# A two-block transformer on one core: two PSUM banks by turns for one accumulation

## The reference

```python
x = x + gt1 * merge_branches(ya, yb, ga, gb, w_pa, w_pb, w_o)   # m @ w_out: 1024 -> 1024
x = x + gt2 * swiglu(h2, w_gate, w_up, w_down)                  # 2816 -> 1024
...                                                             # the second block:
h = h + mix @ w_out[l]
h = h + (silu(gu[..., :D_FF_2]) * gu[..., D_FF_2:]) @ w_down[l]
```

## Time and profile before

| | |
|---|---|
| median of 3 runs | 3452.6 us (3451.89 to 3452.65) |
| span of the profiled execution | 3452.2 us |
| TensorE busy | 3307.5 us, 96% |
| VectorE busy | 1771.3 us, 51% |
| ScalarE busy | 1203.1 us, 35% |
| GpSimd busy | 445.2 us, 13% |
| read from memory | 285.42 MB, 83 GB/s over the span |

### The profile page before, as it was taken

The page is one execution under the profiler, slowest core; times in us unless marked ns, Lnnn a source line. Parts: engine busy times, 40 slices in busy tenths (PEclk is TensorE's granted clock), DMA queues, the critical chain, the costliest instruction groups (busy, mean ns, idle before and its releaser), DMA issues. The chain is left out here.

```text
span 3452.2 us, 49601 instructions
## 1 busy us (share of the span) xinstructions
PE 3307.5 (96%) x20432; PEld 2652.1 (77%) x20432; DVE 1771.3 (51%) x2736; ACT 1203.1 (35%) x2054; POOL 445.2 (13%) x477
## 2 busy tenths in 40 slices
PE   6999999999999999999999999999999998899998
PEld 4887778788888787776887867667888777578886
DVE  5874657654132456655323357654443385744433
ACT  3214762321131222753223333353332332532322
POOL 0211111000000021114500133120000022200000
PEclk9999999999999999999999999999999999999999
DMA  6420013354122122012222321012223220022232
GB/s 243 147 99 18 2 50 141 129 188 141 62 68 68 55 86 68 2 50 89 97 92 94 102 84 58 26 43 92 96 94 104 98 86 3 31 98 92 96 100 80
DMA packets 78265, 290.66 MB, mean 84 GB/s; under 512 B 8672, under 2 KB 9056, under 8 KB 77280
## 3 DMA queue, kind: packets, MB, share of 16 engines
q1 hardware_dynamic: 78048, 287.55, 24.5%
HBM read 285.42 MB, written 2.10 MB: 83 GB/s over the span
## 5 line engine op out<-in xcount | busy, mean ns | idle before, releaser
L459 DVE TENSOR_TENSOR w_low<-ring,w_high 128x1024 fp32r<-128x1024 f32 x418 | 526.7, 1260 | 1351.8 <-ACT w_high L456 1351.2
L494 PE MATMUL ps<-arena_r,w_high 128*128 128x512 f32 x3568 | 1142.1, 385 | 11.1 <-PEq L1517 9.2
L456 ACT ACTIVATE w_high<-ring 128x1024 fp32r<-128x1024 f32 x418 | 442.9, 1060 | 1517.9 <-PE ps L494 1508.8
L494 PEld LDWEIGHTS ps<-arena_r,w_high 128*128 128x128 f32 x3568 | 646.1, 188 | 163.7 <-issue 16.7
L494 PE MATMUL ps<-low,w_high 128*128 128x512 f32 (+1 forms) x2448 | 764.7, 361 | 0.0
L494 PE MATMUL ps<-high,w_high 128*128 128x512 f32 x2368 | 737.0, 362 | 15.0 <-DVE low L992 7.0
L494 PE MATMUL ps<-high,w_low 128*128 128x512 f32 x2368 | 730.7, 359 | 0.0
L494 PE MATMUL ps<-arena_r,w_low 128*128 128x512 f32 (+1 forms) x1456 | 545.6, 387 | 0.0
L494 PEld LDWEIGHTS ps<-low,w_high 128*128 128x128 f32 x2448 | 411.7, 189 | 74.8 <-issue 1.1
L494 PEld LDWEIGHTS ps<-high,w_high 128*128 128x128 f32 x2368 | 395.2, 188 | 95.8 <-issue 12.0
L494 PEld LDWEIGHTS ps<-high,w_low 128*128 128x128 f32 x2368 | 395.0, 188 | 70.3
(11 more groups left out here) (353 smaller groups left out, 2905.8 us busy)
## 6 DMA issues: line engine op xcount, KB each, us to landing
ring<-in_weights SPq DMA_DIRECT2D x428, 512.0 KB, 3.3
arena<-in_ada_rows SPq DMA_DIRECT2D x80, 512.0 KB, 3.9
arena<-in_ada SPq DMA_DIRECT2D x16, 512.0 KB, 15.5
arena<-in_cond_rows SPq DMA_DIRECT2D x3, 1024.0 KB, 5.8
xL<-in_x SPq DMA_DIRECT2D x1, 2048.0 KB, 10.9
out<-xL SPq DMA_DIRECT2D x4, 512.0 KB, 2.7
low_f<-in_low_rank SPq DMA_DIRECT2D x3, 512.0 KB, 4.2
const<-in_const SPq DMA_DIRECT2D x1, 1104.0 KB, 5.4
```

Of the source, the lines that this page charges most:

```text
L456: act.activation(w_high[:, slot, :], ring[:, place, :], ACT.Copy).then_inc(unit_high.sem, 1)
L459: dve.tensor_tensor(w_low[:, slot, :], ring[:, place, :], w_high[:, slot, :].bitcast(F32), ALU.subtract).then_inc(unit_free.sem, 1)
L494: mm = pe.matmul(bank(4 * (t % 2) + 2 * p + s, width), w, g.split[k][s][x], start=(n == 0 and m == 0), stop=(n == len(part) - 1 and m == 2))
```

## The change

In a `Residual` stage with tokens alone the flag `two_sums` is set. Each tile's products then go by turns into the tile's first bank and the one behind it (0 and 1, or 4 and 5): `turn` counts products times three, the first product in each bank starts an accumulation and the last two end the two. VectorE adds the first bank to the stream as before, waits for that instruction through its chain semaphore, and adds the second bank in the same way. `left_v` is raised by the second.

```diff
                 for m, (w, x) in enumerate(((hi_w, 1), (hi_w, 2), (lo_w, 1))):
+                    if g.two_sums:
+
+                        turn = 3 * n + m
+                        mm = pe.matmul(bank(4 * (t % 2) + 2 * p + turn % 2), w, g.split[k][0][x],
+                                       start=(turn < 2), stop=(turn >= 3 * len(part) - 2))
+                        continue
                     for s, width in g.segs:
...
                     g.made, g.own = made, 0 if made else len(g.split)
+                    g.two_sums = evict.two_sums and len(g.segs) == 1
...
         class Evict:
+            two_sums = False
...
         class Residual(Evict):
+            two_sums = True
...
                     ins = dve.scalar_tensor_tensor(x, bank(4 * (c % 2) + s, w), gate, x, ALU.mult, ALU.add)
+                    if g.two_sums:
+                        chain_v.link(dve, ins)
+                        ins = dve.scalar_tensor_tensor(x, bank(4 * (c % 2) + 1), gate, x, ALU.mult, ALU.add)
                 ins.then_inc(left_v.sem, 1)
```

## The result

The changed kernel takes 3458.8 us (median of 21 runs, 3453.23 to 3463.12) against 3451.75 us (21 runs, 3448.31 to 3456.46): 1.0020 times the time before, 95% interval 1.0014 to 1.0027. That is +7.05 us, at the very edge of what was called no change. The forecast was 3457.0 us and +4.4 us, counted from 3452.6 us, the median of the first three runs.

The account below looks back on a forecast made before the run. TensorE, busy 96% of the span, was taken as the bound; pace 0, inner tiles 0 and stage ends 0.78 + 0.78 + 2.1 + 0.73 = 4.4 us on 3452.6 gave 3457.0 us, range 3442 to 3463.

Parts of the forecast that it names:

- no change: Whole kernel: a difference within about 0.2%, 6.9 us; the forecast of +0.13% fell here, chance 0.67.
- Pace unchanged: TensorE in the six stages: switching banks adds 0 per matmul, tile periods stay 5.60 and 15.40 us.
- Steady alternation saves: Rival, 2160 matmuls: 6 to 7 ns less each, 3443 us (chance 0.12), or all 20 ns, 3414 us (0.03).
- steady alternation costs: Rival, 2160 matmuls: accumulation starts in another bank add up to 2 ns each, 3461.3 us or more; chance 0.16.
- The surplus of the pairs of the earlier trace: Token-and-context matmuls alternating banks: about 13 ns surplus each in place of 20, hinting at a 15 us gain.
- Second evictions of the inner tiles free: Tiles 0 to 6, 42 of 48 added evictions: hidden beside matmuls, cost 0; 30 us if uncovered.
- The six ends: Last tile of each changed stage: second eviction delays what follows, 0.78 + 0.78 + 2.1 + 0.73 = 4.4 us.
- the three straight ends: Second block, TensorE going straight into the next stage: late operands of k = 6 and 7, +0.70 us each.
- the program's end: After the last down projection, final norm and output follow the second eviction in one chain: +0.73 us.
- L1105's wait: TensorE's wait for GpSimd after layer 1's down projection: 2.28 us before, expected to become 3.1 us.
- The clock: Rival: longer TensorE idling after layer 1's down projection brings 1.2 GHz, some 2 us, 3460 us; chance 0.02.
- the likeliest case: Whole kernel: matmul pace unchanged and all stage ends paid, 3457.0 us, by itself 3454.5 to 3459.5; chance 0.59.

Follow-up runs that it names:

- the kernel with the banks alone: Changed kernel with products alternating between two banks but the second bank never added to the stream: 3452.49 us, ratio 1.0000.
- the halves: Kernel before, each six-stage matmul split into two of 256 columns: 3458.29 us in one bank, 3451.37 us by turns, beside 3448.91 us.
- the filler: Changed kernel plus three unread matmuls in TensorE's idle time, two before the final norm, one before layer 1's norm: 3457.47 us, ratio 1.0014.
- the order that removes it: Changed kernel; at four ends VectorE does last-tile evictions and two low operand parts before splitting the next stage's second weight unit: 3453.27 us, ratio 1.0001.

## Why the prediction was right, point by point

*Pace unchanged.* Right, and for the reason given: the switch at a tile's end in the trace before was the experiment in small. Periods to the hundredth, and the kernel with the banks alone at a ratio of 1.0000. "Steady alternation saves" (0.15 together) and "steady alternation costs" (0.16) are both refuted. The surplus of the pairs of the earlier trace rows, the one argument for a gain, was smaller per matmul because their matmuls are shorter, as the halves show, and not because the bank changes. The Trainium skill's N / 2.4 + 2.5 ns ("TensorE: Matmul & The Clock Gate", Back-to-back issue gap), which that section calls the gap of an isolated matmul, gives an estimate of 109.2 ns for 256 columns. The traces have 116.7, with or without a change of bank, so what it leaves out is not the bank.

*Second evictions of the inner tiles free.* Right: no cost for 42 of 48 (ratio 1.0000, 0.9991 to 1.0009).

*The six ends, 4.4 us.* Right as a mechanism, and in size by its readings: 0.79 us at layer 1's norm (first distance with the filler), 0.77 us at its down projection, 0.70 us at each of the three straight ends (0.70 forecast; 0.68 and 0.72 by the table), 0.72 us at the program's end where the clock held. That the stall sits behind VectorE's weight split is shown by the order that removes it. One sign was misread: I expected L1105's wait (now L1111) to grow to 3.1 us. It stayed at 2.26, since the stall before k = 6 and 7, 0.39 us idle and slower restarts, falls into the same stretch and uses it up.

*The clock.* This is the term that was mis-sized. I gave it 0.02 and called it small, by one idle gap of 0.64 us around 1614 that had done no harm. Measured are 0.56 us at layer 1's norm in each of six profiles, in a stretch that begins at that very place, 0.9 to 1.7 us at the end in three of six, and a mean clock lower by 0.0009. At the place that I had named for it, layer 1's down projection, the clock is low before as well (0.90 in the 35 us from 1990 us before, 0.91 after). The page's slices of 86 us, on which I leaned, can't show a stretch of a few us.

*A term that was missing.* The instructions of VectorE in layer 1's norm took 0.2 to 0.5 us longer beside GpSimd, at full clock. The sum had priced this end as a shift of an unchanged chain.

With the chains, 4.4 + 0.56 + about 0.3 + half of 1.6 us are some 6.1 us of the 7.05. The rest was not separated; it is small against the interval of the difference (4.8 to 9.3 us).

*Class and range.* +7.05 us lies just beyond the 6.9 us that I took for the bound of no change; the likeliest case's own range (3454.5 to 3459.5) held the time, but partly by luck. The difference was 2.6 us larger than its sum, and the forecast had started from a median of three runs that was 0.85 us above that of the 21.

## What to carry to other kernels

Before trying to hide a per-instruction surplus, find in the old trace an instance of the one thing the edit changes (here a switch of bank, through two tile lengths and two equations), and what the surplus scales with. Work that is free in the middle of a stage is paid in full in its last tile, where the next stage's operands hang on it; price ends one by one, allow for the clock that a longer idle stretch may cost, and look at what stands ahead of the last eviction in the engine's own order. A time that fits is not yet a cause: cut the stretch in two at the moment when the clock falls, and see how much was lost before it. When an experiment fails, read its trace before dropping the theory: it may have moved a second instruction.

## What the runs showed of the hardware

- The columns of these rounded float32 matmuls take 0.456 ns each at full clock (233.3 ns for 512, 116.7 for 256), not 0.417, whatever the number of matmuls, weight loads or banks in these stages; the pairs of 512 and 256 columns took 346.7 ns, 0.451 ns per column.
- With halves into one bank the down projections of the second block took 15.55 us per tile, 0.15 us more than by turns, while all other stages were equal. One run; the cause wasn't sought.
- A second eviction of 0.75 us in the last tile before layer 1's norm was followed by a stretch at 1.2 GHz in all six profiles that have it, worth 0.56 us, and in none of the seven without. In the one profile with a matmul that nobody reads put into TensorE's wait there, the clock stayed at 2.4 GHz (mean 1.00 instead of 0.93 in the stretch).
- VectorE's instructions L835 and L836 in that norm took 0.92 and 1.06 us in place of 0.69 and 0.98 when GpSimd's work on the positions began earlier beside them; that the one causes the other wasn't tested.
